# Feed-forward tiles of a decoder stack: 512-column matmuls for low and high input together, or 256-column matmuls into one half bank

## The reference

```python
def swiglu(h, w_in, w_out):
    a, b = jnp.split(h @ w_in, 2, axis=-1)
    return (jax.nn.silu(a) * b) @ w_out

for l in range(DEPTH):                                   # DEPTH = 2
    h = rms_norm(x, ffn1_norm_pre[l])
    x = x + 0.5 * rms_norm(swiglu(h, ffn1_w_in[l], ffn1_w_out[l]), ffn1_norm_post[l])
    ...                                                  # token mixer
    h = rms_norm(x, ffn2_norm_pre[l])
    x = x + 0.5 * rms_norm(swiglu(h, ffn2_w_in[l], ffn2_w_out[l]), ffn2_norm_post[l])
```

## Time and profile before

| | |
|---|---|
| median of 3 executions | 1733.29 us (1733.17 to 1736.93) |
| the profiled execution | 1733.12 us, of which the span from first to last instruction is 1731.0 us |
| PE, matmuls | 1700.1 us busy (98%), 10546 instructions |
| PE, weight loads | 1487.8 us busy (86%), 10546 |
| DVE | 1252.3 us busy (72%), 2290 |
| ACT | 960.9 us busy (56%), 1622 |
| DMA engines | 180 GB/s on the mean |

### The profile page before, as it was taken

One profiled execution on the slowest core, in us unless ns is written; L12 is line 12 of the kernel. 1 busy time (PEld: TensorE's weight loads), 2 busy tenths in 40 slices (PEclk: granted clock), 3 DMA queues, 4 the chain that ended last, 5 costly groups with the idle time before them and its releaser, 6 DMA issues.

```text
span 1731.0 us, 28424 instructions
## 1 busy us (share of the span) xinstructions
PE 1700.1 (98%) x10546; PEld 1487.8 (86%) x10546; DVE 1252.3 (72%) x2290; ACT 960.9 (56%) x1622; POOL 22.2 (1%) x21
## 2 busy tenths in 40 slices
PE   7999999999999999999999999999999999989998
PEld 6888899998888888888899988888888988878887
DVE  6666777568876677666777567866677789796875
ACT  5544564566555546444655565554556555573574
POOL 1000000000000000000000000000000000000000
PEclk9999999999999999999999999999999999999999
DMA  7544554535455554544555535444554444313531
GB/s 302 200 187 182 189 215 186 226 147 195 172 194 185 195 202 174 201 184 182 188 216 193 219 123 217 185 183 182 187 213 150 189 172 175 117 38 146 200 129 61
DMA packets 29904, 311.59 MB, mean 180 GB/s; under 512 B 3312, under 2 KB 3696, under 8 KB 4848
## 3 DMA queue, kind: packets, MB, share of 16 engines
q1 hardware_dynamic: 28944, 307.13, 47.2%
q0 software_dynamic: 864, 3.15, 0.6%
HBM read 309.21 MB, written 1.05 MB: 179 GB/s over the span
## 4 chain that ended last, share of the span: by engine, by line
PE 91%; DVE 5%; issue 2%; ACT 1%; DMA 1%; DVEq 0%; SPq 0%; ACTq 0%
PE psum L931 88%; PE psum L938 3%; DVE ring_r L519 1%; DMA ring<-in_weights 0%; DVE PTs L3121 0%; PE psum L1360 0%; DVE Sb L2602 0%; DVE PTs L3111 0%; DVE region L2804 0%; DVE x L2447 0%; ACT region L1974 0%; DMA cst<-in_const 0%; ACT Sb L1849 0%; DVE xs L2384 0%; DVE xs L2400 0%
## 5 line engine op out<-in xcount | busy, mean ns | idle before, releaser
L513 ACT ACTIVATE region_r<-ring 128x1024 fp32r<-128x1024 f32 x505 | 524.7, 1054 | 352.5 <-PE psum L931 333.1
L519 DVE TENSOR_TENSOR ring_r<-ring,region_r 128x1024 fp32r<-128x1024 f32 x496 | 591.5, 1220 | 127.9 <-ACT region_r L513 123.1
L931 PE MATMUL psum<-xs_r,region_r 128*128 128x256 f32 (+2 forms) x3160 | 581.2, 331 | 1.8 <-ACT region_r L513 1.2
L931 PEld LDWEIGHTS psum<-xs_r,region_r 128*128 128x128 f32 (+1 forms) x3160 | 467.6, 188 | 63.6 <-issue 8.1
L931 PE MATMUL psum<-region_r 128*128 128x512 f32 (+3 forms) x1056 | 331.3, 382 | 0.0
L931 PE MATMUL psum<-xs_r,ring_r 128*128 128x256 f32 x2344 | 317.7, 278 | 0.0
L931 PEld LDWEIGHTS psum<-xs_r,ring_r 128*128 128x128 f32 x2344 | 303.9, 188 | 15.8
L931 PE MATMUL psum<-region_r,xs_r 128*128 128x512 f32 (+2 forms) x1056 | 267.0, 348 | 2.2 <-ACT xs_r L1890 1.2
L931 PEld LDWEIGHTS psum<-region_r 128*128 128x128 f32 (+2 forms) x1056 | 193.0, 185 | 36.4 <-DVE region_r L2475 0.6
L931 PEld LDWEIGHTS psum<-region_r,xs_r 128*128 128x128 f32 x1056 | 185.1, 190 | 29.0 <-ACT xs_r L1890 3.0
L931 PE MATMUL psum<-ring_r,region_r 128*128 128x512 f32 (+1 forms) x472 | 169.4, 375 | 0.0
(11 more groups left out here) (253 smaller groups left out, 1536.5 us busy)
## 6 DMA issues: line engine op xcount, KB each, us to landing
ring<-in_weights SPq DMA_DIRECT2D x192, 1536.0 KB, 6.2
gpost<-in_posts POOLq DMA_DIRECT2D x6, 512.0 KB, 3.9
cst<-in_const SPq DMA_DIRECT2D x1, 1165.0 KB, 22.6
PTs<-in_mem SPq DMA_DIRECT2D x1, 1024.0 KB, 5.5
x<-in_x SPq DMA_DIRECT2D x1, 1024.0 KB, 8.0
out<-x SPq DMA_DIRECT2D x2, 512.0 KB, 2.6
pars<-in_par SPq DMA_DIRECT2D x1, 368.0 KB, 6.0
p<-in_par SPq DMA_DIRECT2D x1, 206.0 KB, 22.6
```

The costliest lines, as they stand in the source:

```text
L513: eng.activation(unit.high, unit.like_high(unit.raw), ACT.Copy).then_inc(h_ready, 1)
L519: eng.tensor_tensor(unit.like_high(unit.low), unit.like_high(unit.raw), unit.high.bitcast(F32), ALU.subtract)\
L931: ins = pe.matmul(bank, lhsT, rhs, start=start, stop=stop)
```

## The change

wide_tile is gone. Gate and value tiles call split_tile, into the left half of their bank, so each kk has two matmuls of 256 columns in place of one of 512, and the bank holds the finished sum. ACT takes Silu straight from the gate's bank and frees it; DVE multiplies it with the value's bank and frees that. The copies, the two additions and the semaphore half_ready go. Silu now waits until the value's bank was freed by the product two tiles before, which had read the same half of sil; the product waits for the gate's bank to be freed (Silu done) and the value's to be full. The rest of the diff renumbers the counts of the semaphore g_steps.

```diff
-            def split_tile(job, half, u, signal, it=0):
+            def split_tile(job, half, u, signal, it=0, between=None):
                 unit = Split(u, it)
                 to = job.bank[:, half * SEQ:(half + 1) * SEQ].rearrange("p (i t) -> p i t", i=NT)
                 pe.wait_ge(h_ready, unit.count)
                 for kk in range(KD):
+                    if kk == 3 and between is not None:
+                        between()
                     w = unit.high[:, kk * P:(kk + 1) * P]
                     mm(to, w, hH[:, :, kk, :], kk == 0, False)
                     mm(to, w, hL[:, :, kk, :], False, False)
                 pe.wait_ge(l_ready, unit.count)
                 for kk in range(KD):
                     mm(to, unit.low[:, kk * P:(kk + 1) * P], hH[:, :, kk, :], False, kk == KD - 1,
                        signal if kk == KD - 1 else None)
-            def wide_tile(job, u, signal, it=0, between=None):
-                unit = Split(u, it)
-                to = job.bank.rearrange("p (c t) -> p c t", c=2 * NT)
-                pe.wait_ge(h_ready, unit.count)
-                for kk in range(KD):
-                    if kk == 3 and between is not None:
-                        between()
-                    mm(to, unit.high[:, kk * P:(kk + 1) * P], h_both[:, kk, :, :], kk == 0, False)
-                pe.wait_ge(l_ready, unit.count)
-                for kk in range(KD):
-                    mm(to[:, NT:2 * NT, :], unit.low[:, kk * P:(kk + 1) * P], hH[:, :, kk, :], False, kk == KD - 1,
-                       signal if kk == KD - 1 else None)
@@ up_gate
-                    wide_tile(job, u, job.full, it, between)
+                    split_tile(job, 0, u, job.full, it, between)
@@ up_value
-                    wide_tile(job, at + (3 * t if t else 1), job.full, it)
+                    split_tile(job, 0, at + (3 * t if t else 1), job.full, it)
@@ silu
                     gate_.wait_full(act_)
-                    act_.activation(halves[:, t % 2, 0, :], gate_.bank[:, 0:SEQ], ACT.Copy).then_inc(half_ready, 1)
-                    gate_.wait_emptied(act_)
-                    act_.activation(sil[:, t % 2, :], gT[:, t % 2, :], ACT.Silu).then_inc(sil_ready, 1)
-                    job.wait_full(act_)
-                    act_.activation(halves[:, t % 2, 1, :], job.bank[:, 0:SEQ], ACT.Copy).then_inc(half_ready, 1)
+                    job.wait_empty(act_)
+                    act_.activation(sil[:, t % 2, :], gate_.bank[:, 0:SEQ], ACT.Silu).then_inc(gate_.free, 1)
@@ gated
-                    dve.wait_ge(half_ready, 2 * parts_made(f, t, it) - 1)
-                    dve.tensor_tensor(g, halves[:, t % 2, 0, :], gate_.bank[:, SEQ:2 * SEQ], ALU.add).then_inc(gate_.free, 1)
-                    dve.wait_ge(sil_ready, before + 1)
-                    dve.wait_ge(half_ready, 2 * parts_made(f, t, it))
-                    dve.tensor_tensor(g, halves[:, t % 2, 1, :], job.bank[:, SEQ:2 * SEQ], ALU.add).then_inc(job.free, 1)
+                    gate_.wait_emptied(dve)
+                    job.wait_full(dve)
+                    dve.tensor_tensor(g, sil[:, t % 2, :], job.bank[:, 0:SEQ], ALU.mult).then_inc(job.free, 1)
                     job.wait_emptied(dve)
-                    dve.tensor_tensor(g, sil[:, t % 2, :], g, ALU.mult).then_inc(g_steps, 1)
-                    dve.wait_ge(g_steps, 2 * before + 1)
                     dve.tensor_copy(high, g).then_inc(g_steps, 1)
```

More of the change, by code:

```diff
@@ L734, in build @@
         yH_ready, yL_ready = sem("yH_ready"), sem("yL_ready")
-        g_steps, gL_ready, half_ready = sem("g_steps"), sem("gL_ready"), sem("half_ready")
-        halves = PTflat[:, 0:4 * SEQ].rearrange("p (t n s) -> p t n s", t=2, n=2)
+        g_steps, gL_ready = sem("g_steps"), sem("gL_ready")
         mH_ready, mL_ready = sem("mH_ready"), sem("mL_ready")
@@ L2461, in gated @@
                     gate_, job = (Job(name, f, t, plus=2 * it) for name in ("ff", "fu"))
-                    before = lay[0] * (2 * FT) + it * SLOTS + (f * FT + t)
+                    steps = lay[0] * (2 * FT + NT) + it * SLOTS + (f * (FT + NT) + t)
                     g = gT[:, t % 2, :]
                     high, low = gated_parts(f, t)
-                    dve.wait_ge(half_ready, 2 * parts_made(f, t, it) - 1)
-                    dve.tensor_tensor(g, halves[:, t % 2, 0, :], gate_.bank[:, SEQ:2 * SEQ], ALU.add).then_inc(gate_.free, 1)
-                    dve.wait_ge(sil_ready, before + 1)
-                    dve.wait_ge(half_ready, 2 * parts_made(f, t, it))
-                    dve.tensor_tensor(g, halves[:, t % 2, 1, :], job.bank[:, SEQ:2 * SEQ], ALU.add).then_inc(job.free, 1)
+                    gate_.wait_emptied(dve)
+                    job.wait_full(dve)
+                    dve.tensor_tensor(g, sil[:, t % 2, :], job.bank[:, 0:SEQ], ALU.mult).then_inc(job.free, 1)
                     job.wait_emptied(dve)
-                    dve.tensor_tensor(g, sil[:, t % 2, :], g, ALU.mult).then_inc(g_steps, 1)
-                    dve.wait_ge(g_steps, 2 * before + 1)
                     dve.tensor_copy(high, g).then_inc(g_steps, 1)
-                    dve.wait_ge(g_steps, 2 * before + 2)
+                    dve.wait_ge(g_steps, steps + 1)
                     dve.tensor_tensor(low, g, high.bitcast(F32), ALU.subtract).then_inc(gL_ready, 1)
@@ L2479, in first_gated @@
                     job = Job("ff", f, i)
-                    dve.wait_ge(sil_ready, lay[0] * (2 * FT) + (f * FT + i) + 1)
+                    dve.wait_ge(sil_ready, lay[0] * NT + i + 1)
                     dve.tensor_tensor(gT[:, i, :], sil[:, i, :], job.bank[:, SEQ:2 * SEQ], ALU.mult).then_inc(job.free, 1)
@@ L2485, in first_parts @@
                     job = Job("gT", i)
-                    before = lay[0] * (2 * FT) + (f * FT + i)
+                    steps = lay[0] * (2 * FT + NT) + FT + 2 * i
                     cols = slice(i * P, (i + 1) * P)
@@ L2490, in first_parts @@
                         dve.tensor_copy(gH[:, t, cols], job.bank[:, t * P:(t + 1) * P]).then_inc(g_steps, 1)
-                    dve.wait_ge(g_steps, 2 * before + 2)
+                    dve.wait_ge(g_steps, steps + 2)
                     dve.tensor_tensor(gL[:, :, cols], job.bank[:, 0:SEQ].rearrange("p (t n) -> p t n", t=2),
```

## The result

The changed kernel takes **1739.79 us** (median of 7 runs, 1738.36 to 1742.36) against 1733.29 (7 runs, 1732.35 to 1736.94): 1.0037 times the time before, 95% interval 1.0027 to 1.0046. It is slower by 6.5 us, and 1740.7 was forecast. The profiled execution took 1738.59 us, with a span of 1736.8 us, 5.8 more than before.

The account below looks back on a forecast made before the run. It took PE's matmul starts to bound the feed-forward. Matmuls +7.9 and the stall -0.3, with output products, ACT and DVE 0, gave +7.6 us on the profiled 1733.12: 1740.7 us, range 1731.0 to 1746.3.

Parts of the forecast that it names:

- What bounds the kernel: Feed-forward: PE is busy throughout, so a block lasts as long as its matmuls take to start one after another.
- Matmuls, +7.9: Gate and value tiles: 48 matmuls at 117.8 ns, 5.65 us a period against 5.56, +7.9 us over 84 periods.
- two paces that a stretch keeps and the entry that decides: 256-column matmuls run at 113.3 or 117.8 ns; a stretch keeps the one that it enters with.
- Output products, 0: Feed-forward output products, unchanged but entered from another pace: taken as 0, bounds -1.3 and +5.6 us.
- The lower bound, -1.3 us: Output products: all twelve at the pace of the last eight, 226 ns each, -0.015 a period.
- ACT and DVE, 0: Gating: copies and additions go, yet the relief is worth nothing; ACT idles until PE frees places, and nothing waits for DVE's chain.
- The stall, -0.15 a layer: End of the first feed-forward: two matmuls take 0.60 us where 0.45 is usual; the shorter chain removes that, -0.3 in all.
- The fast pace: Rival: the gate tile enters behind the output products at 113.3 ns, -10.2 - 0.3, 1722.6 us; chance 0.17.
- the entry behind the memory values: Mixer: a split tile behind 512-column products runs at the slow pace from its first tile; gate tile's 117.8 ns taken from it.
- The mixed pace: Rival: one tile of a period slow, the other fast, -0.01 a period, 1731.6 us; chance 0.09 with the even case.
- the range: Whole kernel: from the mixed case, 1731.0, to the slow pace with slow output products, 1746.3 us; fast case left out.
- only the starts cost: Rival: high part pays 2.5 ns for each of 16 pairs, low weights stay at 114.4; +3.4, 1736.2 us; chance 0.07.

Follow-up runs that it names:

- fast_entries: Kernel before with one_wide_first's gate tile, value tile by split_tile with product straight from its bank, mixer entered as in mixer_entered_wide: 1722.56 us against 1732.94; again 1723.62 against 1732.83.
- split_two_halves: Kernel before with each 512-column matmul of gate and value tiles cut into two of 256, one per half bank, gating unchanged: 1740.43 us against 1733.08.
- one_wide_first: As split_two_halves, but the first of the gate tile's eight matmuls (kk = 0) stays 512 columns wide: 1727.61 us against 1733.08 for the kernel before.
- mixer_entered_wide: Kernel before with one more 512-column matmul, its result overwritten, ahead of the mixer's first tile in each layer: 1731.36 us against 1732.94.
- one_wide_middle: As one_wide_first, but the 512-column matmul stands fifth (kk = 4) in the gate tile: 1740.80 us against 1733.36 for the kernel before.
- relief_alone: Kernel before with the new Silu and product but the old 512-column matmuls; high weights by low input left out of the result: 1732.71 us against 1733.08.
- gate_entered_wide: Changed kernel with one more 512-column matmul, its result overwritten, ahead of each gate tile: 1743.03 us against 1732.83 for the kernel before.
- input_shifted_64: Changed kernel with the input tile moved in SBUF, by 64 elements in place of 16: 1758.63 us against 1733.08 for the kernel before.

## Why the prediction was right, step by step

*What bounds the kernel.* Right: PE stayed busy through the feed-forward. The periods give +6.7 us; the profiled span grew by 5.8. Between the two, to some tenths: the end of the first feed-forward, -0.2 in each layer; a first gate tile that starts at 30.15 us in place of 31.15, -1.0; and the mixers, +1.6 in layer 1 and -1.2 in layer 2. That these nearly cancel is luck. The early start isn't the change's: the two profiles of fast_entries start at 30.20 and 30.65. At the span's start the matmuls of one product start 427 ns apart and then 216, and in the profile before five more of them are slow. Of the mixers' two differences, 1.2 us each is a single wait of PE, for a high part that ACT makes. It stands in layer 1 after the change (the first two lines; ACT had waited for the weights' transfer) and in layer 2 before it (the third):
```profile
314.51 2.00 ACT L513 ACTIVATE region_r<-ring 128x1024 fp32r<-128x1024 f32 x2 [3.78 <-DMA ring<-in_weights]
315.71 2.12 PE L930 MATMUL psum<-xs_r,region_r 128*128 128x256 f32 x16 [1.16 <-ACT region_r L513]
```
```profile
955.68 2.07 PE L931 MATMUL psum<-xs_r,region_r 128*128 128x256 f32 x16 [1.18 <-ACT region_r L513]
```
Of fast_entries, one profile has this wait (1.22 us) and one has not, so it need not be the change's.

*Matmuls, +7.9.* Right in place and size: +0.09 a period, at 117.7 ns in place of 115.8. split_two_halves shows that they carry the change by themselves. The reading behind it, two paces that a stretch keeps and the entry that decides, is shown for 256 columns by one_wide_first and mixer_entered_wide: one matmul at the entry turns 46 or 336 fast. It was incomplete in what an entry is: a 512 alone is none (one_wide_middle); it has to be the first behind the 512-column products at 227 ns, where a 256 leads into the slow pace. In this light the kernel before had its low weights near the quicker pace (114 to 115), and the change took away the wide matmuls that led into it. Its 512s, 233 ns on the mean, are at twice neither pace, so for them the two paces explain nothing yet.

*Output products, 0.* Small miss in size: -0.015 a period (2.720 for 2.735 us, from single starts), -1.3 us in all. They too depend on what went before. Behind tiles at 117.7 ns they are at 227 ns from the first (108.56 to 108.79); behind tiles at 113.3 the first takes 231 (one_wide_first). The lower bound, -1.3 us, is what came.

*ACT and DVE, 0.* Right: relief_alone. *The stall, -0.15 a layer.* It went as said, and the output products behind it in that block run at 227 too, so it was about -0.2.

*The rivals.* The fast pace is real in this form (gate_entered_wide), but the gate tile doesn't enter it behind the output products: the entry behind the memory values was the right row to read it from. The mixed pace did not occur. (The sum of that case gives 1731.6 us; the range, which is said to start from it, starts at 1731.0. Nothing hangs on it.) That only the starts cost is out: at the fast pace two matmuls take 2 x 113.3 = 226.6 ns, less than the 233.1 of the one that they replace. The Trainium skill's gap for isolated matmuls (TensorE: Matmul & The Clock Gate, Back-to-back issue gap), N/2.4 + 2.5 ns, makes two starts dearer than one always, and for 256 columns it gives 109 ns, by an estimate from that page. The runs have 113.3, 117.7 and 119.8, so the measurement decides.

*What stays open.* Why there are two paces, and why a 256 behind the output products ends in the slow one. input_shifted_64 shows that the input's address in SBUF bears on it; which reads of PE meet, no run here shows.

## What to carry to other kernels

Where PE is busy throughout, take the price of a matmul form from the distance of starts in that form, behind the same predecessor; one column count can have several prices. Look at the first starts of a stretch behind each kind of predecessor: if they settle on two levels, one matmul at the entry may be worth trying, even one whose result is thrown away. Work taken off ACT and DVE, which wait for PE here, brought nothing (relief_alone).

## What was not expected of the hardware

An added matmul can save time (mixer_entered_wide: 0.23 us paid, 1.48 gained). Moving a tile by 48 elements in SBUF cost 18.8 us (input_shifted_64 against the changed kernel). And stretches behind other work settle on either pace from one profile to the next, in the very same kernel. A late mixer tile of fast_entries, in its two profiles, 24 matmuls ahead of L938's:
```profile
1659.28 2.10 PE L931 MATMUL psum<-xs_r,region_r 128*128 128x256 f32 x16
1661.21 1.07 PE L931 MATMUL psum<-xs_r,ring_r 128*128 128x256 f32 x8
1662.12 0.82 PE L938 MATMUL psum<-cst,Sb 128*128 128x128 f32 x6
```
```profile
1660.87 2.15 PE L931 MATMUL psum<-xs_r,region_r 128*128 128x256 f32 x16
1662.86 1.11 PE L931 MATMUL psum<-xs_r,ring_r 128*128 128x256 f32 x8
1663.80 0.82 PE L938 MATMUL psum<-cst,Sb 128*128 128x128 f32 x6
```
Eight low-weight matmuls take 0.91 us in the one and 0.94 in the other, 114 and 118 ns. The two profiles are of two chips, so whether chip or execution decides is open.

Such a tile is worth a tenth of a us. The 2 to 5 us by which executions of one kernel differ here go mostly with the granted clock: one_wide_first took 1723.34 and 1724.26 us at a mean clock of 1.000, and 1727.61 to 1728.36 at 0.998. What a fall costs can be read from a tile of the first mixer, in the first and second profile of fast_entries, the second with its window (columns as in the earlier trace rows):
```profile
315.04 2.08 PE L931 MATMUL psum<-xs_r,region_r 128*128 128x256 f32 x16
```
```profile
317.00 3.57 PE L931 MATMUL psum<-xs_r,region_r 128*128 128x256 f32 x16
317.00:320.40 3.40, 3.40 (x19) 3.40 (x19) 0.00 (x0) 0.91 (x4) 0.00 (x0) 0.53 0.67 282
```
There the clock is 0.53 on the mean, near the lower level of 1.2 GHz, most starts are 213 ns apart in place of 113 to 118, and the tile of 24 takes 1.6 us longer. Just before it, from 314.00 on, PE had been busy 2.31 of 3.00 us, with the clock at 1.00. The first profile has such a stretch in layer 2, at 950.73.
